# The first RMSNorm of a hybrid decoder layer: its factor leaves the matmul operands and is applied to the products

## The chip, the core and the metric

The kernel runs on one core of a Trainium2 chip. The core has a matrix engine (TensorE, PE in the profile, with PEld for its weight loads), three engines for elementwise work (VectorE or DVE, ScalarE or ACT, GpSimd or POOL) and SyncE (SP), which here issues every DMA. The engines run their own instruction streams and wait for each other by semaphores. The metric is the device time of one execution in microseconds, lower is better. The kernel's matmuls are in fp32r; for accuracy each fp32 product is made from three of them, with each operand split into a high part (rounded to fp32r) and a low part (the rest): high x high, high x low, low x high.

## What is computed

One layer of a decoder for 1088 tokens (1024 of a prompt, 64 of samples), model width 1024. Cut to the part that the change touches:

```python
h = rmsnorm(x, norm1_g)                  # x * rsqrt(mean(x*x) + EPS) * g, per token
z = h @ w_in                             # columns: c_q 384 | c_kv 256 | k_rope 32 | u 512 | v 512
c_kv = rmsnorm(z[..., 384:640], kv_norm_g)
k_r = rope(z[..., 640:672], pos)
q = rmsnorm(z[..., :384], q_norm_g) @ w_q_up
zg = gelu(z[..., 672:])                  # u and v, exact GELU
u = zg[..., :512]
v = layernorm(zg[..., 512:], v_norm_g, v_norm_b)
g = u * (w_s @ v + b)                    # per chunk of 128 tokens, causal
# attention on q, c_kv, k_r; merge, w_out, residual, second norm, SwiGLU, final norm
```

Everything behind these lines is the same in both kernels. `c_kv`, `k_r` and the samples' `v` are outputs too.

## The kernel before

**Layout.** `x1` holds x with the model width on the partitions: 128 partitions x 8 blocks (`KD`) x 1088 tokens. The tokens come in four column groups, `CH1` = 128, 256, 384 and 320 tokens. `hH`/`hL` are the high and low parts of h in the same layout. They are the stationary operands of the v and u products and the moving ones of the rest. `vwH`/`vwL` and `uwH`/`uwL` are the split weights of v and u.

**Norm 1 in the kernel before.** For each group c: ACT squares the group into `sq0` (line 1557). PE adds the squares over the partitions with a matmul against `ones` (`sum_squares`, line 947), which leaves each token's sum in all partitions of PSUM bank 4+c. DVE picks the diagonal (2068), reduces it (2076) and makes mean plus EPS (2078). POOL raises it to -0.5 (`power`, 739). DVE makes diagonal matrices of the factors (2087), and PE spreads them over the partitions (`spread`, 955). DVE then scales each block of x by gain and factor in place (2058), ACT rounds it into `hH` (1548) and DVE subtracts into `hL` (2116).

**The v stage.** PE makes nine token tiles t = 0 to 8 (128 tokens, the last 64); each is 8 blocks of 3 matmuls (lines 939 to 941, 128x512), 24 in all, into bank t % 4. Tile 0 follows the four weight pieces: `w_v` comes in four loads of 512 KB through `raw`, a ring of two slots; POOL rounds a piece into `vwH` (724), DVE subtracts into `vwL` (2102), and the slot's next load waits for that. Tile t >= 4 waits until the GELU of tile t-4 has left its bank. ACT makes the GELU (1596); DVE the statistics (2139 to 2143); POOL the power (780); DVE the LayerNorm (2149 to 2154); ACT the high part `vH`, POOL the low part `vL` (791). Each engine's program is a loop over t with this order written by hand. Into it are set: the spatial weights on POOL at t = 1 (767 to 727), norm 1 of the fourth group on ACT and DVE at t = 2, and the four pieces of the u weights (`U_SPLITS`: at t = 2, 3, 4, 4, POOL then DVE).

**Behind it.** The u stage has the same nine tiles with `uwH`/`uwL`; its tile 0 waits for the GELU of v tile 5, its tile 1 for that of v tile 6, and so on, and for its weight pieces. The spatial matmuls (`spatial`) stand behind u tile 3. The z stage multiplies six weight pieces (`w_in`: c_q, c_kv, k_rope) with `hH`/`hL`, and normalises c_q and c_kv by the same scheme of sums, `columns`, `power` and `diagonals` as norm 1. Then come attention, the output projection, the gated product in loops (Strassen-like, the bulk of the time), and the final norm.

**SP's queue** is one program as well. It issues loads in a written order and waits in it: whatever stands behind a waiting load waits with it.

## Time and profile before

| | us |
|---|---|
| median of 3 runs | 1373.38 |
| lowest and highest run | 1372.34, 1375.17 |
| span of the profiled execution | 1370.6 |
| PE busy in it | 1319.6 (96%) |
| DVE busy in it | 841.9 (61%) |
| first v product of PE | 15.77 |
| first u product of PE | 84.17 |

The span is the profiler's, from first to last instruction; the device time of a run holds a little more at both ends (here 2.8 us to the median). A row of a timeline gives start, duration, engine, line, operation, output<-input, shape, count and, in brackets, the engine's idle time before it and what ended it. Durations of matmuls overlap: the distance of two starts is what one costs in a row of them.

### The profile page before, as it was taken

What the parts mean: (1) busy time and instruction counts of PE and PEld (TensorE: products, weight loads), DVE (VectorE), ACT (ScalarE), POOL (GpSimd) and SP (SyncE); (2) the same over time, 40 slices, a digit from 0 to 9 for tenths busy, and PEclk for the clock granted to TensorE, in tenths of its full rate; (3) what the DMA queues carried; (4) which work ended last, traced back from release to release, by engine and by line L of the source; (5) the groups of instructions that cost most, each with busy time, mean ns of one, the idle gap of its engine ahead of it and who ended that gap; (6) DMA issues with size and microseconds to landing.
All of it is one profiled execution on the core that took longest, in us unless ns stands there. A gap on an engine that the chain in (4) does not pass through costs nothing.

```text
span 1370.6 us, 24016 instructions
## 1 busy us (share of the span) xinstructions
PE 1319.6 (96%) x9436; PEld 1234.7 (90%) x9436; DVE 841.9 (61%) x1284; ACT 508.4 (37%) x886; POOL 432.3 (32%) x279
## 2 busy tenths in 40 slices
PE   6999999999999999899999999999999999999997
PEld 4778998788888667899899999999999999999987
DVE  5896136666666336447965534455445568998976
ACT  3413223665665414112522222222222234544461
POOL 1362333633423204654044444444443410000000
PEclk9999999999999899999999999999999999999998
DMA  7001001100005643642122222222221279757503
GB/s 250 16 31 66 32 31 41 39 1 21 0 19 181 213 173 112 209 149 86 39 80 79 86 72 72 69 77 86 78 86 64 78 276 352 261 190 239 183 1 131
DMA packets 67771, 146.34 MB, mean 107 GB/s; under 512 B 7810, under 2 KB 15362, under 8 KB 67234
## 3 DMA queue, kind: packets, MB, share of 16 engines
q1 hardware_dynamic: 67682, 145.12, 31.2%
q8 instruction: 59, 0.97, 0.3%
q14 instruction: 30, 0.25, 0.1%
HBM read 122.54 MB, written 22.55 MB: 106 GB/s over the span
## 4 chain that ended last, share of the span: by engine, by line
PE 81%; DVE 9%; issue 4%; DMA 2%; ACT 2%; POOL 2%; SPq 0%; POOLq 0%; DVEq 0%; ACTq 0%
PE ps L939 24%; PE ps L940 24%; PE ps L941 24%; PE ps L1179 2%; DMA araw<-in_w_dn 1%; PE ps L947 1%; DVE x L2058 1%; PE ps L1245 1%; POOL rt L739 1%; PE ps L1290 1%; DVE diag L2087 1%; DVE mL L2409 1%; PE ps L955 1%; PE ps L1255 1%; DVE aHL L2720 0%
## 5 line engine op out<-in xcount | busy, mean ns | idle before, releaser
L908 POOL TENSOR_TENSOR ws<-wraw,ws 128x1024 fp32r<-128x1024 f32 x50 | 125.3, 2506 | 214.9 <-ACT ws L1548 214.9
L939 PE MATMUL ps<-bHL,aHL 128*128 128x272 f32 x616 | 178.4, 290 | 4.3 <-DVE bHL L2723 4.1
L941 PE MATMUL ps<-bHL,aHL 128*128 128x272 f32 x616 | 177.3, 288 | 0.0
L940 PE MATMUL ps<-bHL,aHL 128*128 128x272 f32 x616 | 177.1, 288 | 0.0
L2566 DVE TENSOR_TENSOR bufP<-bufP,ps 128x544 f32<-128x544 f32 x66 | 47.4, 720 | 131.9 <-PE ps L941 129.6
L1548 ACT ACTIVATE ws<-wraw 128x1024 fp32r<-128x1024 f32 x55 | 58.4, 1062 | 173.1 <-PE ps L941 169.0
L939 PEld LDWEIGHTS ps<-bHL,aHL 128*128 128x128 f32 x616 | 116.0, 188 | 5.6 <-DVE bHL L2723 5.5
L940 PEld LDWEIGHTS ps<-bHL,aHL 128*128 128x128 f32 x616 | 116.0, 188 | 0.0
L941 PEld LDWEIGHTS ps<-bHL,aHL 128*128 128x128 f32 x616 | 115.9, 188 | 0.0
L931 POOL TENSOR_TENSOR rt<-ms,mhalf 128x3 f32<-128x3 f32 (+1 forms) x3 | 3.0, 997 | 252.7 <-DVE ms L2753 252.7
L2299 DVE TENSOR_TENSOR pTL<-ps,pTH 128x512 fp32r<-128x512 f32 (+1 forms) x96 | 53.2, 555 | 43.3 <-ACT pTH L1548 42.3
L908 POOL TENSOR_TENSOR ws<-wsum,ws 128x1024 fp32r<-128x1024 f32 x20 | 57.3, 2865 | 60.5 <-ACT ws L1548 60.5
L1548 ACT ACTIVATE aHL<-araw 128x512 fp32r<-128x512 f32 x66 | 41.7, 632 | 91.9 <-DVE araw L2695 47.3
L848 POOL TENSOR_TENSOR prob<-prob,rsm 128x128 f32<-128x128 f32 (+5 forms) x48 | 49.6, 1042 | 77.7 <-DVE rsm L2274 77.7
L2566 DVE TENSOR_TENSOR bufC<-bufP,ps 128x544 f32<-128x544 f32 x42 | 30.2, 719 | 69.1 <-PE ps L941 69.1
L1548 ACT ACTIVATE pTH<-ps 128x512 fp32r<-128x512 f32 (+1 forms) x96 | 46.9, 489 | 49.0 <-PE ps L1179 48.0
L1712 ACT ACTIVATE prob<-ps,nmx 128x128 f32<-128x128 f32 (+3 forms) x64 | 47.4, 740 | 24.1 <-DVE nmx L2285 23.9
L2285 DVE TENSOR_REDUCE nmx<-ps 128x1 f32<-128x128 f32 (+3 forms) x64 | 47.7, 751 | 12.6 <-PE ps L1160 12.2
L939 PE MATMUL ps<-x5H,ws 128*128 128x272 f32 x176 | 50.8, 289 | 2.0 <-DVE x5L L2481 1.6
L1179 PE MATMUL ps<-ident,prob 128*128 128x128 f32 x288 | 50.2, 285 | 2.5 <-DVE pTL L2299 1.0
L939 PE MATMUL ps<-x3H,ws 128*128 128x272 f32 x176 | 50.8, 289 | 0.9 <-DVE x3L L2476 0.9
L939 PE MATMUL ps<-x1H,ws 128*128 128x272 f32 x176 | 50.8, 288 | 1.0 <-POOL ws L908 1.0
(365 smaller groups left out, 4561.8 us busy)
## 6 DMA issues: line engine op xcount, KB each, us to landing
araw<-in_w_dn SPq DMA_DIRECT2D x121, 256.0 KB, 3.4
wraw<-in_w_gu SPq DMA_DIRECT2D x44, 512.0 KB, 3.6
cp<-in_cache SPq DMA_DIRECT2D x64, 272.0 KB, 4.8
ab<-acts SPq DMA_DIRECT2D x34, 272.0 KB, 4.9
raw<-in_w_out SPq DMA_DIRECT2D x16, 512.0 KB, 4.2
acts<-bufC SPq DMA_DIRECT2D x22, 272.0 KB, 2.1
x<-x2s SPq DMA_DIRECT2D x8, 544.0 KB, 6.5
x2s<-x SPq DMA_DIRECT2D x14, 272.0 KB, 4.7
```

Source lines behind the costliest of these rows:

```text
L739: pool.tensor_tensor(rt[:, j % 4, :], ms[:, j % 4, :], mhalf[:, :].broadcast_to((P, 3)), ALU.pow).then_inc(nm_pow, 1)
L848: pool.tensor_tensor(row, row, rsm[:, r % 4:r % 4 + 1].broadcast_to((P, n)), ALU.mult).then_inc(s_pn, 1)
L908: pool.tensor_tensor(w[:, 1, :], w_source(j), w[:, 0, :], ALU.subtract).then_inc(cw_lo, 1)
L939: nc.tensor.matmul(out, wh, xh, start=start, stop=False)
L940: nc.tensor.matmul(out, wh, xl, start=False, stop=False)
L941: return nc.tensor.matmul(out, wl, xh, start=False, stop=stop)
L1179: last = nc.tensor.transpose(ps[:, 4 + x % 2, P * qi:P * qi + P], prob[:, at:at + P], ident[:, :])
L1548: return nc.scalar.activation(out, x, ACT.Copy, scale=scale)
L1712: nc.scalar.activation(prob[:, prob_at(qt):prob_at(qt) + n], psf[:, 1024 * (r % 2):1024 * (r % 2) + n], ACT.Exp, bias=nmx[:, s:s + 1], sca ...
L2285: nc.vector.tensor_reduce(nmx[:, s], psf[:, at:at + P * (qt + 1)], AX.X, ALU.max, negate=True).then_inc(s_nm, 1)
L2299: nc.vector.tensor_tensor(pTL[:, x % 4, c0:512], ps[:, 4 + x % 2, c0:512], pTH[:, x % 4, c0:512], ALU.subtract).then_inc(t_free, 1)
L2566: nc.vector.tensor_tensor(halves(out[:, g, :]), halves(x[:, g, :]), pair(b + 2 * g), ALU.add).then_inc(added, 1)
```

## The change

1. **Operands.** `hH` and `hL` are now the two parts of x * g without the token's factor r = rsqrt(mean + EPS). ACT rounds x * g with the gain as its scale (`hi1`); DVE makes the low part with one `scalar_tensor_tensor`, x * g - hH (`low1`). Squares, sums, picks, diagonals and spreads of norm 1 are gone from ACT, PE, DVE and POOL, and so is the scaling pass.
2. **Factor.** A second copy of x in DRAM, `x_tok` (1088 x 1024, tokens on the partitions), is loaded in ten pieces of 512 KB (the ninth overlaps the eighth, the tenth holds the 64 samples, 256 KB) through `xt`, a ring of three slots. ACT squares a piece and adds it up by row (`square_rows`, with `accum_out`) into `ssq1`; DVE makes mean plus EPS in four batches (`mean1`: pieces 0, 1-2, 3-5, 6-9); POOL makes the power (`power1`) into `rv1`, tokens on the partitions.
3. **Where it is applied.** The GELUs of v and u take `rv1` as their per-partition scale. The norms of c_q and c_kv cancel the factor, if EPS is divided by r squared: `columns` adds `eq1` = EPS * q1 instead of EPS. For the key, `rv1` is stored to DRAM (`r_row`, 1088 elements of 4 bytes) and loaded back over 64 partitions (`csr`), where DVE multiplies it by the rotary table `cs`; the key uses `csr`.
4. **Order.** SP's loads stand in another order, ACT's loop has the squares in it, the gelu table is loaded earlier in ACT's program. PE has no norm-1 work in the v stage.
5. Small things: `ident` is loaded with the constants; some semaphores are merged; `dynamic_dma_scratch_size=1024` is given to the builder.

```diff
+XT = 10
+XT_AT = [*range(0, SEQ, P), T - P, SEQ]
+XT_BATCH = (0, 1, 3, 6, XT)
...
+def xt_rows(b):
+    return min(P, T - XT_AT[b])
+def xt_of(t):
+    return t if t < NT - 1 else XT - 1
...
+            def load_xt(b):
+                if b >= 3:
+                    sp_.wait_ge(n1_sq, b - 2)
+                m = xt_rows(b)
+                sp_.dma_start(xt[0:m, b % 3, :], d["x_tok"][XT_AT[b]:XT_AT[b] + m, :]).then_inc(ld_xt[b % 3], 16)
...
+            sp_.wait_ge(n1_pow, len(XT_BATCH) - 1)
+                sp_.dma_start(r_row[0:SEQ].rearrange("(j p) -> p j", p=P), rv1[:, 0:SEQ // P]).then_inc(ld_cs, 16)
+                sp_.dma_start(r_row[SEQ:T].rearrange("(j p) -> p j", p=NS), rv1[0:NS, XT - 1:XT]).then_inc(ld_cs, 16)
             sp_.wait_ge(v_fin, NT)
             sp_.dma_start(d["v_out"], vs[0:NS, :]).then_inc(out_v, 16)
+            sp_.wait_ge(ld_cs, 32)
             sp_.dma_start(cs[:, :], d["cs"]).then_inc(ld_cs, 16)
+            sp_.dma_start(csr[NOPE:P, :], r_row[:].unsqueeze(0).broadcast_to((P - NOPE, T))).then_inc(ld_cs, 16)
...
+            def power1(b):
+                cols = slice(XT_BATCH[b], XT_BATCH[b + 1])
+                pool.wait_ge(n1_mean, b + 1)
+                pool.tensor_tensor(rv1[:, cols], q1[:, cols],
+                                   mhalf[:, :].broadcast_to((P, cols.stop - cols.start)), ALU.pow).then_inc(n1_pow, 1)
...
                 split(N_V + j, gw(vwH, j), None)
-                if j == 0:
-                    power(J_N1)
-            power(J_N1 + 1)
-            power(J_N1 + 2)
-            fold(J_N1 + 3, sq0, KD // 2, CH1[3][1], 0)
-            power(J_N1 + 3)
+            power1(0)
+            power1(1)
...
+                if t == 2:
+                    power1(2)
+                elif t == 4:
+                    power1(3)
...
-            sum1(0)
-            spread1(0)
             for t in range(NT):
                 m, b = rows(t), t % 4
-                if t == 2:
-                    sum1(3)
-                elif t == 4:
-                    spread1(3)
...
-                    if t == 0 and k == KD // 2:
-                        sum1(1)
-                    elif t == 1 and k == KD - 2:
-                        spread1(2)
...
-                if t == 0:
-                    spread1(1)
-                    sum1(2)
...
+            def square_rows(b):
+                m = xt_rows(b)
+                act.wait_ge(ld_xt[b % 3], 16 * (b // 3 + 1))
+                nc.scalar.activation(xt[0:m, b % 3, :], xt[0:m, b % 3, :], ACT.Square,
+                                     accum_out=ssq1[0:m, b:b + 1]).then_inc(n1_sq, 1)
...
+                    act.wait_ge(n1_pow, sum(at <= xt_of(t) for at in XT_BATCH))
+                    nc.scalar.activation(v_tile(t), ps[0:m, t % 4, :], ACT.Gelu,
+                                         scale=rv1[0:m, xt_of(t):xt_of(t) + 1]).then_inc(v_gelu, 1)
...
+            low1(0, range(2))
             weights_lo(N_V, gw(vwL, 0), gw(vwH, 0))
-            factors1(0)
-            norm1(0)
-            for j in range(2, 4):
+            low1(0, range(2, KD))
+            for j in range(1, 4):
                 weights_lo(N_V + j, gw(vwL, j), gw(vwH, j))
-            for c in range(1, 3):
-                factors1(c)
-                norm1(c)
-            factors1(3)
+                if j == 1:
+                    low1(1, range(4))
+                elif j == 2:
+                    low1(1, range(4, KD))
+            low1(2)
+            mean1(0)
+            mean1(1)
...
+            dve.wait_ge(ld_cs, 64)
+            nc.vector.tensor_tensor(csr[NOPE:P, :], csr[NOPE:P, :], cs[NOPE:P, :], ALU.mult).then_inc(kr_a, 1)
```

How the written order moves, at three places. **DVE, the start of the program, before** (`vwL` is a weight piece's low part, `x_102` is `x1`, `g_52` the gain):

```order
L2102 TENSOR_TENSOR vwL<-raw,vwH 128x1024
L2068 TENSOR_TENSOR diag<-ps,ident 128x128
L2076 TENSOR_REDUCE sums<-diag 128x1
L2078 TENSOR_SCALAR ms<-sums 128x1
L2087 TENSOR_TENSOR diag<-ident,rt 128x128
L2058 SCALAR_TENSOR_TENSOR x_102<-x_102,g_52,ps 128x128 x2
L2116 TENSOR_TENSOR hL<-x_102,hH 128x128
```

The same place in the changed kernel (`x_107` is `x1`):

```order
L2136 SCALAR_TENSOR_TENSOR hL<-x_107,g_52,hH 128x128 x2
L2130 TENSOR_TENSOR vwL<-raw,vwH 128x1024
L2136 SCALAR_TENSOR_TENSOR hL<-x_107,g_52,hH 128x128 x6
L2130 TENSOR_TENSOR vwL<-raw,vwH 128x1024
L2136 SCALAR_TENSOR_TENSOR hL<-x_107,g_52,hH 128x256 x4
L2130 TENSOR_TENSOR vwL<-raw,vwH 128x1024
L2136 SCALAR_TENSOR_TENSOR hL<-x_107,g_52,hH 128x256 x4
```

The first two low parts of h stand ahead of the first weight piece now, the factor's steps are gone, and the second group's low parts stand between the weight pieces.

**SP, the start of its program, before:**

```order
L506 DMA x_102<-in_x 128x8x128
L510 DMA ident<-in_ident 128x128
L510 DMA g_52<-in_g 128x8
L502 DMA raw<-in_w_v 128x1024 x2
L506 DMA x_102<-in_x 128x8x256
L506 DMA x_102<-in_x 128x8x384
L502 DMA raw<-in_w_v 128x1024 x2
L519 DMA vgb<-in_vgb 128x1024
```

The same place in the changed kernel:

```order
L524 DMA x_107<-in_x 128x8x128
L534 DMA g_52<-in_g 128x8
L520 DMA raw<-in_w_v 128x1024 x2
L524 DMA x_107<-in_x 128x8x256
L520 DMA raw<-in_w_v 128x1024 x2
L524 DMA x_107<-in_x 128x8x384
L531 DMA xt<-in_x_tok 128x1024 x3
L524 DMA x_107<-in_x 128x8x320
```

The third and fourth weight pieces moved ahead of the third group of x, and three pieces of the token-major copy stand ahead of the fourth group and of all constants.

**ACT, the loop of the v stage, before** (`vf` is a GELU's output):

```order
L1596 ACTIVATE vf<-ps 128x512 x2
L1548 ACTIVATE hH<-x_102 128x320 x8
L1548 ACTIVATE cmaskR<-cmask 128x128
L1548 ACTIVATE identR<-ident 128x128
L1596 ACTIVATE vf<-ps 128x512
L1548 ACTIVATE vH<-vf 128x512
```

The same place in the changed kernel (`rv_77` is `rv1`, `ssq_75` is `ssq1`):

```order
L1584 ACTIVATE xt,ssq_75<-xt 128x1024 x3
L1618 ACTIVATE vf<-ps,rv_77 128x512 x2
L1568 ACTIVATE hH<-x_107,g_52 128x320 x8
L1618 ACTIVATE vf<-ps,rv_77 128x512
L1568 ACTIVATE vH<-vf 128x512
L1584 ACTIVATE xt,ssq_75<-xt 128x1024 x3
L1618 ACTIVATE vf<-ps,rv_77 128x512
```

Three row squares stand ahead of the first GELU, three ahead of the fourth, and four (not shown) ahead of the sixth.

## Rows read from the trace of the kernel before

**Rows 1.** The page's first part: busy time, share of the span, instructions.

```profile
PE 1319.6 (96%) x9436; PEld 1234.7 (90%) x9436; DVE 841.9 (61%) x1284; ACT 508.4 (37%) x886; POOL 432.3 (32%) x279
```

**Rows 2.** The chain that ended last, its first 16 us: start, us, what.

```profile
2.71 5.62 DMA raw<-in_w_v
8.50 1.06 POOL vwH L724
9.69 1.23 DVE vwL L2102
...
15.34 0.29 DVE hL L2116
```

**Rows 3.** The timeline of PE, 0 to 85 us: start, us, engine, line, operation.

```profile
6.72 3.75 PE L947 MATMUL ps<-sq,ones 128*128 128x128 f32 x16 [6.72 <-ACT sq L1557]
...
15.77 0.77 PE L939 MATMUL ps<-vwH,hH 128*128 128x512 f32 x1 [1.20 <-DVE hL L2116]
...
16.34 0.63 PE L940 MATMUL ps<-vwL,hH 128*128 128x512 f32 x1
...
20.60 0.63 PE L941 MATMUL ps<-vwH,hL 128*128 128x512 f32 x1
...
21.80 3.78 PE L947 MATMUL ps<-sq,ones 128*128 128x256 f32 x16 [0.57 <-DVE vwL L2102]
...
40.76 0.94 PE L955 MATMUL ps<-diag,ones 128*128 128x128 f32 x6 [2.60 <-DVE diag L2087]
...
56.59 0.48 PE L939 MATMUL ps<-vwH,hH 128*128 128x512 f32 x1
...
84.17 0.39 PE L939 MATMUL ps<-uwH,hH 128*128 128x512 f32 x1
```

**Rows 4.** Busy time of lines 947 and 955, 0 to 60 us, summed.

```profile
sum 60.00, PE 15.18 PEld 10.98; mean PE 3.04 PEld 2.20
...
sum 60.00, PE 3.27 PEld 2.59; mean PE 0.65 PEld 0.52
```

**Rows 5.** Groups by form, 0 to 84 us, and timeline rows of POOL, ACT, DVE.

```profile
L2154 DVE TENSOR_TENSOR vf<-vf,vgb 128x512 f32<-128x512 f32 x4 | 5.7, 1430 | 0.1
L2102 DVE TENSOR_TENSOR uwL<-raw,uwH 128x1024 fp32r<-128x1024 f32 x3 | 5.8, 1943 | 0.0
L1548 ACT ACTIVATE hH<-x 128x384 fp32r<-128x384 f32 x8 | 4.2, 526 | 6.8 <-DVE x L2058 6.8
L2058 DVE SCALAR_TENSOR_TENSOR x<-x,g,ps 128x320 f32<-128x320 f32 x8 | 4.2, 534 | 0.0
...
59.43 2.51 POOL L727 TENSOR_TENSOR spL<-raw,spH 128x1024 fp32r<-128x1024 f32 x1
...
77.79 0.58 ACT L1596 ACTIVATE vf<-ps 128x512 f32<-128x512 f32 x1
...
83.67 0.58 ACT L1596 ACTIVATE vf<-ps 128x512 f32<-128x512 f32 x1
...
104.73 1.66 DVE L2154 TENSOR_TENSOR vs<-vs,vgb 64x512 f32<-64x512 f32 x1
```

**Rows 6.** DMA: one stretch of 3 us (last two columns share, GB/s); a wait; a landing.

```profile
12.00:15.00 3.00, 0.79 (x2) 0.50 (x2) 1.51 (x3) 0.01 (x1) 1.59 (x2) 1.00 1.07 377
...
18.04 1.05 POOL L724 TENSOR_SCALAR vwH<-raw 128x1024 fp32r<-128x1024 f32 x1 [4.45 <-DMA raw<-in_w_v]
...
raw<-in_w_u SPq DMA_DIRECT2D x4, 512.0 KB, 3.6
```

**Rows 7.** The timeline of ACT: its first square, 1024 columns, behind the load of x.

```profile
5.52 1.06 ACT L1557 ACTIVATE sq<-x 128x1024 f32<-128x1024 f32 x1 [3.44 <-DMA x<-in_x]
```

**Rows 8.** A DMA issue with its landing, POOL's timeline, and DVE in a stretch (0.00).

```profile
x<-in_x SPq DMA_DIRECT2D x1, 512.0 KB, 4.7
...
119.32 1.04 POOL L724 TENSOR_SCALAR w0H<-raw 128x1024 fp32r<-128x1024 f32 x1
...
160.00:180.00 20.00, 20.00 (x124) 20.00 (x123) 0.00 (x0) 4.75 (x7) 3.84 (x3) 1.00 0.15 53
```

220 lines of the change are left out of this document (114 added, 106 removed).

## The prediction, made before the changed kernel was run

> **What bounds the kernel now.** I read the busy shares first: PE is busy for 96% of the span, DVE for 61% [rows 1]. So a change pays if it takes work or waiting from PE's own stream, and what happens on the other engines counts only where PE waits for them. Then I read the chain that ended last and PE's timeline in the part that the change touches. In the chain [rows 2] the first weight piece lands, is rounded and has its low part at 9.69 + 1.23 = 10.9 us, but PE's first product starts only at 15.77 [rows 3]: between lie diagonal, power, spread and scaling, the norm's factor. In PE's timeline the sums (line 947) and spreads (955) of norm 1 stand between the products, 15.18 and 3.27 us of busy time [rows 4], with one more wait of 2.60 us for a diagonal [rows 3]. From 56.59 to the first u product at 84.17 there is nothing but products: 5 tiles of 24 in 27.58 us, 5.52 us a tile, 0.230 us a product. From there into the z stage PE hardly waits in its timeline, and what follows in the u and z stages is timed by what PE has done. So I need one number: when the first u product starts. The rest of the kernel moves by the same amount.
>
> **Start of PE.** The two parts of x * g need only the first group of x and g. The load of x lands at 5.5 [rows 7]; two high and two low parts, each under the 0.53 us of the wider ones [rows 5], are ready by 7.6, before the weights. So the first product starts when the first weight piece is ready: 10.9, say 11.0, which is 4.8 us earlier.
>
> **Tile 0** takes its products in four portions of 6, one per weight piece. The early products before cost (20.60 - 16.34) / 10 = 0.426 us each [rows 3], against 0.230 later: the first at TensorE's lower clock level (1.2 GHz), the later ones at the upper (2.4), though the granted clock is given as 1.00 for an early stretch too [rows 6]. Portion 1: 11.0 to 13.6. The second piece landed with the first; DVE makes six low parts (an estimate of 0.34 each for 128 columns, from 0.534 for 320 [rows 5]; 2.0 us), then the piece (1.23 [rows 2]): ready at 14.2 at the latest. Portion 2: 14.2 to 16.8. The third piece is issued when its slot is free (10.9). Before, it landed only at 18.0 [rows 6], behind 2.5 MB of x at up to 377 GB/s; now the third group of x stands behind it, and I take the 3.6 us of a piece that has the queue to itself [rows 6]: 14.5. POOL 1.05 to 15.6; DVE, behind four low parts of 256 columns (an estimate of 0.47 by the same row), ready at 17.3. The fourth piece, issued at 14.2, lands at 17.8, POOL to 18.9, DVE behind four more low parts to 20.4. Portion 4 then ends at 21.8 at the upper level, 23.0 at the lower. With the low parts overlapping a little (0.1 us each) it would be 21.1. I take 21.7.
>
> The row shows that 3.75 us of work at the lower level, from 6.72, did not raise the clock, and that it stood at the upper level from about 22, after products from 15.77 on. The Trainium skill ("TensorE: Matmul & The Clock Gate", Part 1) says that a throttled clock is the default and that sustained matmul activity releases it; by that the small gaps between my four portions could hold it down longer. The sum would be 1.2 us worse for portion 4, and up to 2.5 more if the next tile's first dozen are slow too.
>
> **Tiles 1 to 8.** Tile 1 needs the second group (low parts done at 19.2), tile 3 the third, tile 6 the fourth. No norm work stands between them: 8 x 5.52 = 44.2 us if nothing is late. First u product: 21.7 + 44.2 = **65.9**, against 84.17: 18.3 us earlier. Cross-check by what leaves PE: behind 15.77 stood 15.18 - 3.75 of sums and 3.27 - 0.79 of spreads, 13.9 us, and 2.6 us of waiting; tile 0 costs about 10.7 now where its products alone cost 12 x 0.426 + 12 x 0.230 = 7.9. 13.9 + 2.6 - 2.8 = 13.7, with 4.8 of the start 18.5. The two agree.
>
> **Is something late?** Loads: the third group of x is issued behind the fourth weight piece at 14.2 and lands at about 21.5 at 370 GB/s; ACT's 8 high parts (0.53 each [rows 5]) are done at 25.5, DVE's low parts at 26, tile 3 needs them at 32.7. Three pieces of the token-major copy land by 25.7, the fourth group by 29.5, the constants by 32. ACT squares a piece in 1.06 us [rows 7]: three until 28.5. Batch means and powers (0.9 us each) are done by 29.5; the GELU of tile 0 is at 28, of tile 1 at 30. PE needs them at 38.3 and 43.8. The fourth group (ACT from 29.5) is ready on DVE by 40.5; it was 7.0 us of scaling and subtracting, now 8 instructions that lie near the 0.534 of the 320-wide one [rows 5]; tile 6 needs it at 49.3.
>
> The tightest chain is the one through all engines. Pieces 3 to 5 of the copy are issued from 26, behind them the spatial weights, which land at about 37.5. POOL works on these until 43.5, 2.51 us of it in one instruction [rows 5]; DVE's instructions with two SBUF inputs stretch beside such work (a weight piece at line 2102 takes 1943 ns on average [rows 5] and 1.23 us with POOL idle [rows 2]; line 2154 takes 1430 [rows 5]), which I count. DVE ends tile 1's norm at 44.8 and the first u piece at 46.5, then comes the third mean (46.7), POOL's power (47.6) and the GELU of tile 3 at 48.3: PE needs it at 54.8, 6 us of room. DVE then needs what it needed before, 5.88 us for a tile and a u piece by the distance of two GELUs that waited for it (77.79 and 83.67 [rows 5]). ACT reaches the last four squares at about 52.6; the tenth piece is issued behind the seventh square, lands at 56.5, and the GELU of tile 5 ends at 58.6. The first u product waits for it at 65.9: 7 us. The fourth u piece is ready at 61.6, needed at 70.0. The GELU of tile 6 waits for the last power (62.6), needed at 71.4. So the program has 6 to 8 us of room at each meeting, and PE should wait nowhere. DVE ends the LayerNorms at about 79.5 where it was 104.73 + 1.66 = 106.4 [rows 5]; the spatial products need them at 87.7.
>
> **What is added later.** The row squares, ten of 1.06 us plus an accumulator read, are on ACT, which has the room. The store of `r_row` waits for the last power (62.6) behind all u loads; `csr` and `cs` come behind v's last norm (79.5) and ahead of the six w_in pieces. POOL takes the first w_in piece at 119.32 before [rows 8], so at 101 now: nothing there unless the store takes over 30 us. The product for `csr` (1088 columns, under the 1430 ns x 2 of two stretched instructions of 512 [rows 5]) lies in DVE's idle time; DVE was wholly idle from 160 to 180 [rows 8]. The norms of c_q and c_kv change one short instruction of 3 columns into another: between -0.1 and +0.1 us on each of six links, taken as zero. The GELU's scale from a column instead of a constant: its 0.58 us [rows 5] could become 0.5 to 0.7, beside PE's work, so zero.
>
> The Trainium skill ("DMA: Bandwidth & Descriptors", Specifications) asks for transfers of at least 512 B for line rate and has shorter ones do a read-modify-write. No row here has a four-byte run; the rule gives no price, and by the sum above it moves nothing while the store is within its room.
>
> **Sum.** 1373.38 - 18.4 (between the two countings, 18.3 and 18.5) = **1355.0 us**. Against the profiled execution: 1370.6 - 18.4 = 1352.2 of span, plus the 2.8 us that lie around it.
>
> **Rivals.**
> - *The factor comes late.* The chain of tile 3's or tile 5's GELU through loads, squares, mean and power is later than its room of 6 to 8 us. For: it crosses five engines and a ring of three slots, each of my times is a sum of some ten terms, and DVE was behind PE in this stage before: the GELU of tile 5 started at 77.79 [rows 5], 6.4 us ahead of its need at 84.17. Against: DVE loses its scaling pass. Being 9 to 12 us late gives the first u product at 68 to 71: 1357 to 1361.
> - *A better start.* The clock rises early and the pieces come quickly: tile 0 ends at 20.5, 1353.8; if in addition waits in the z stage happen to close, 1352.5.
> - *The gain is given back.* The u or z stage is bound by an engine that kept its own time. For: DVE ended the v stage only at 106.4, 22 us behind the first u product. Against: that end moves by 27 us, more than PE. It would give 1360 to 1370; at its end the change doesn't do what it says, and the factor's work only sits elsewhere.
> - *Slower, by the store of `r_row`.* 1088 runs of four bytes, and SP waits for them with the w_in pieces behind. The nearest row is the first load of x, 1024 runs of 512 B in 4.7 us [rows 8]. If the store took over 42 us, POOL would hold the powers of the u stage behind a missing w_in piece, and PE would lose one for one; from 63 us on the kernel is slower. At 70 ns a run, 76 us, it would be 1355 + 34 = 1389. That is sixteen times the row's price.
>
> **Chances.** Forecast (1353.5 to 1357) 0.70; late factor 0.14; better start 0.06; given back 0.07; slower 0.03. A difference of 0.2%, 2.7 us, is about what a measurement of this kernel tells from none: faster 0.95, same 0.02, slower 0.03. The range takes in the better start and the late factor, and leaves out about 0.12: 1352.5 to 1361.
>
> **What would show it.** Right: first product at 11, tile 0 done by 22, first u product near 66, no wait of PE over 1 us between, DVE's last LayerNorm near 80, and PE's busy time 18 us less. Wrong: PE waiting for an ACT GELU at 49 to 72 us (the late factor), products at 0.43 us behind 24 us (the clock), a wait for `w0H` at 124 (the store), or an unchanged start of attention.

## The result, and the profile after

The changed kernel takes 1363.45 us in the median of 4 runs (1359.54 to 1364.8), the kernel before 1373.36 beside it; the ratio is 0.9931, 95% interval 0.9917 to 0.9944. So it is faster, by 9.9 us where 18.4 were forecast, and 2.5 us outside the range. The profiled execution has a span of 1360.7 us (1362.44 with what lies around it). In both kernels 1.7 us lie around the span of a run; the 2.8 us of the table before set the profiled run's span against the time of another run.

PE's busy time, the row that answers to [rows 1], fell from 1319.6 to 1308.5, by 11.1 and not by 18. Second row: the granted clock in 40 slices, in tenths.

```profile
PE 1308.5 (96%) x9362; PEld 1226.2 (90%) x9362; DVE 821.2 (60%) x1241; ACT 513.0 (38%) x902; POOL 429.2 (32%) x279
...
PEclk9999999999999899899999999999999999999998
```

PE's timeline, against [rows 3]. The four rows with an idle time are the starts of tile 0's four portions.

```profile
10.45 0.77 PE L983 MATMUL ps<-vwH,hH 128*128 128x512 f32 x1 [10.45 <-DVE vwL L2130]
...
13.89 0.80 PE L983 MATMUL ps<-vwH,hH 128*128 128x512 f32 x1 [0.55 <-DVE vwL L2130]
...
17.39 0.80 PE L983 MATMUL ps<-vwH,hH 128*128 128x512 f32 x1 [0.57 <-DVE vwL L2130]
...
20.89 0.80 PE L983 MATMUL ps<-vwH,hH 128*128 128x512 f32 x1 [0.57 <-DVE vwL L2130]
...
25.75 0.63 PE L985 MATMUL ps<-vwH,hL 128*128 128x512 f32 x1
26.18 0.45 PE L983 MATMUL ps<-vwH,hH 128*128 128x512 f32 x1
...
68.50 0.39 PE L983 MATMUL ps<-uwH,hH 128*128 128x512 f32 x1
```

The starts are those of the forecast: 11.0, 14.2, 17.3, 20.4 were expected. But twelve products from 20.89 to 26.18 cost 0.44 us each, and only from 26.18 on do they cost 0.227. The first u product stands at 68.50, 15.7 us earlier than before; 65.9 was forecast. PE's waits from 0 to 110 us (in total, times, the longest):

```profile
PE ps L983 <- DVE vwL L2130: 12.1, 4, 10.4
```

So PE waits for nothing but the four weight pieces. The engines behind it (ACT's square and accumulator read, the GELUs of tiles 3 and 5, the last LayerNorm, the first w_in piece, the key's table), in ACT's, DVE's and POOL's timelines:

```profile
28.30 0.18 ACT L1584 ACTIVATION_READ_ACCUMULATOR xt<-xt 128x1 f32 x1
28.39 1.04 ACT L1584 ACTIVATE xt<-xt 128x1024 f32<-128x1024 f32 x1
...
51.61 0.69 ACT L1618 ACTIVATE vf<-ps,rv 128x512 f32<-128x512 f32 x1 [8.90 <-POOL rv L776]
...
62.65 0.67 ACT L1618 ACTIVATE vf<-ps,rv 128x512 f32<-128x512 f32 x1
...
83.75 1.66 DVE L2187 TENSOR_TENSOR vs<-vs,vgb 64x512 f32<-64x512 f32 x1
...
131.03 3.34 DVE L2243 TENSOR_TENSOR csr<-csr,cs 64x1088 f32<-64x1088 f32 x1
...
103.57 1.06 POOL L760 TENSOR_SCALAR w0H<-raw 128x1024 fp32r<-128x1024 f32 x1
```

And the small transfers of the factor, 60 to 100 us (KB each, median us to landing):

```profile
csr<-r_row SPq DMA_DIRECT2D x1, 272.0 KB, 5.5
...
r_row<-rv SPq DMA_DIRECT2D x1, 4.0 KB, 9.5
r_row<-rv SPq DMA_DIRECT2D x1, 0.2 KB, 10.5
```

Where the rest went is read from the starts of the first product of each stage. Stretches in us, first execution of each kernel; "n160" is a kernel of the experiments (`n_fetch160`) that does the work of the changed one:

```
stretch                                          before    after     n160
start to first u product                          84.17    68.50    68.13
u stage and z stage                              146.93   146.87   146.90
to the attention's first probabilities            23.73    24.46    24.48
attention                                        196.71   196.49   196.53
samples, to their first product with the cache    19.62    20.37    18.60
to the output projection                          57.78    57.78    57.79
output projection, to the second norm's sums      60.65    61.65    60.66
second norm, to x0 of the gated product           52.96    52.92    51.36
gated product, x0 to x6                           43.01    43.02    43.02
gated loop, from x6 on                           428.61   429.73   428.63
down projection                                  214.89   217.47   215.22
final norm                                        41.54    41.44    41.39
first u product to the end                      1286.43  1292.20  1284.57
```

The u and z stages took what they took. The changed kernel loses 0.7 at the start of attention, 0.8 in the samples' part, 1.0 in the output projection, 1.1 in the gated loop and 2.6 in the down projection, and gains 0.4 in the others: 5.8 us in all are given back, in stages whose instructions are the same.

### The profile page after: what moved, and what is told of

Same layout as the page of the kernel before. It is cut to its first block, busy times and chain, and to the rows that moved or that the text cites. A ratio compares the mean times of both kernels' runs of the same rounds, so it can differ in the third digit from the quotient of the medians.

```text
span 1360.7 us, 23850 instructions
## 1 busy us (share of the span) xinstructions
PE 1308.5 (96%) x9362; PEld 1226.2 (90%) x9362; DVE 821.2 (60%) x1241; ACT 513.0 (38%) x902; POOL 429.2 (32%) x279
## 4 chain that ended last, share of the span: by engine, by line
PE 80%; DVE 8%; issue 5%; DMA 3%; ACT 2%; POOL 2%; SPq 0%; POOLq 0%; DVEq 0%; ACTq 0%
PE ps L983 24%; PE ps L984 24%; PE ps L985 24%; PE ps L1199 2%; DMA araw<-in_w_dn 2%; PE ps L1265 1%; DVE x L2082 1%; PE ps L991 1%; DMA ab<-acts 1%; PE ps L1310 1%; POOL rt L782 1%; DVE mL L2446 1%; DVE hL L2136 1%; PE ps L1275 1%; DVE aHL L2757 0%
```

## The experiments

All were timed in five rounds, beside runs of the kernel before (medians 1372.3 to 1373.4). "Rest" is the median less the 1.7 us around the span and less the first u product of the kernel's profile. As that product comes from one execution (67.57 to 68.50 in three of the changed kernel), a rest is good to about 1 us.

### The two kernels again, and a frame without the change

**The changed kernel a second and a third time.** (`a_after`, `p_after`)

> The changed kernel again. In its first trace the first u product starts at 68.50 us, 15.7 us earlier than before, but the end comes only 9.9 us earlier: 5.8 us are given back, about 0.7 at the start of attention, 0.6 in the samples' part, 1.1 in the output projection, 1.1 at the start of the gated loop, 2.6 in the down projection. Theory 1 (chance of that one execution: the spells of low clock and DMA landings differ from one execution to the next): the median of more runs is near 1373.4 - 15.7 = 1358 us, between 1357 and 1360, and the shifts of the parts differ in the new trace. Theory 2 (lasting: something of the change costs time late in the program): again 1362 to 1364, and the same parts give the same amounts back.

1363.88 us (6 runs), ratio 0.9934 (0.9914 to 0.9954); first u product 67.57, the stretch behind it 1295.0. The same parts give time back, three of them in other amounts: 0.7 us at the start of attention, 1.1 in the samples' part, 0.7 in the output projection, 2.6 in the gated loop, 3.8 in the down projection.

> The changed kernel unchanged, beside the three others on one chip. Median 1362 to 1365, first u product 67.5 to 68.5, loop entry 429.7 (x6 to the down projection), down projection 217.5 to 218.7, a fetch 1.5 to 1.75 us behind the issue of the load at the loop's entry, which lands after 5.1 to 5.4 us. If it comes out at 1357 here, the differences to the kernels with waits were between chips and not between kernels.

1362.04 us (6 runs), ratio 0.9915 (0.9897 to 0.9933). In three sets, 16 executions in all, the changed kernel's rest is 1292.4 to 1294.6: the loss is lasting. Not all its parts are: the down projection takes 217.5 and 218.7 us in the first two profiles but 216.0 in this one, under what was expected. And single executions last from 1357.16 to 1366.17 us. Their mean granted clock goes with that: it is 0.984 in the seven of 1363.4 to 1366.2 us, 0.985 or 0.986 in the eight of 1359.5 to 1363.4, and 0.989 in the one of 1357.16.

**The kernel before again.** (`a_before`)

> The kernel before again, for a second trace of it: how much the stretches between the same two matmuls differ between two executions of one kernel. Theory 1: single stretches (start of attention, samples' part, output projection, down projection) differ by 0.5 to 2.5 us from the first trace, the time stays at 1373 to 1375 by the median. Theory 2: the stretches repeat within 0.3 us.

1372.92 us (12 runs), ratio 1.0004 (0.9994 to 1.0014), rest 1287.5. Nine of the eleven stretches behind the first u product repeat within 0.3 us; the samples' part is 0.4 us shorter and the output projection 0.7 longer.

**The kernel before with the change's DRAM tensors and scratch size, unused.** (`c_frame`)

```
+        r_row = nc.dram_tensor("r_row", (T,), F32).ap()
-    arr = {"x": ...}
+    arr = {"x": ..., "x_tok": x}
-    nc = bacc.Bacc(...)
+    nc = bacc.Bacc(..., dynamic_dma_scratch_size=1024)
```

> The kernel before with the changed kernel's surroundings alone: the second copy of x and the row of factors exist in DRAM, but nothing loads or stores them, and the builder has the smaller scratch for dynamic DMA. Every engine's instructions are those of before. If the place of the tensors in DRAM or the scratch costs what was given back late, this runs 3 to 6 us slower than before (1376 to 1379). If neither matters: 1373 to 1374.

1372.73 us (12 runs), ratio 0.9998 (0.9987 to 1.0009). Placement in DRAM and scratch size cost nothing. In its profile the first u product stands at 85.33, 1.2 us later than in the kernel before with the same instructions; the clock was low from 13.3 to 20.1 and from 40.6 to 44.0 us.

### The early clock

**Filler products** (`b_warm`; 128x128 of ones into a free bank), 24 before tile 0 and 6 in each weight wait:

```
+            fill(24, 4)
             for t in range(NT):
...
+                        if k:
+                            fill(6, 5)
                         pe.wait_ge(split_lo, N_V + k // 2 + 1)
```

> The changed kernel with matmuls that serve nothing on PE, ones by ones into free banks: 24 ahead of the first v product and 6 in each of the three waits for a weight piece. Clock theory: PE's products in tiles 0 and 1 cost 0.43 us until 26 us because PE had done too little before; kept busy from 1 us on, they cost 0.23 from about 11 us, tile 0 ends near 22.3, and the first u product starts at 66 to 66.5 where it was 68.5; the time falls by 2 to 2.5 us. Rival (the clock follows the time since the start, not the work): products stay at 0.43 until 26, the filling costs 3 x 1 us or more, the first u product is at 70 to 73 and the kernel 2 to 5 us slower than the changed one.

1351.58 us (5 runs), ratio 0.9851 (0.9832 to 0.987). The first u product came at 66.23, as expected. But the total fell by 12.3 us and not by 2.3; its rest is 1283.7. (The profile has two records for each filler.)

**Only the 24 ahead of tile 0:** (`f_head`)

> The changed kernel with only the 24 filler products before tile 0, none in the three weight waits. Those waits (0.55 to 0.57 us each in the changed kernel) come back. If short waits with a quarter of tile 0 between them keep the granted clock at its lower level, the products of tile 0 stay at 0.43 us until about 26 us and the first u product stands at 68 to 68.5; if the early work alone raises it, it stands at 66.5 to 67. Behind it: theory A (shift alone) gives 1292 to 1295 at 68.5 and an open number at 66.5; theory B (early work) gives 1286 in either case. Totals: 1353 for B, 1361 to 1364 for A at 68.5.

1354.02 us (4 runs), ratio 0.9859 (0.9839 to 0.988). PE's timeline of this kernel:

```profile
1.05 8.43 PE L1008 MATMUL ps<-ones 128*128 128x128 f32 x48 [1.05 <-POOL ms L794]
10.17 0.50 PE L983 MATMUL ps<-vwH,hH 128*128 128x512 f32 x1 [0.69 <-DVE vwL L2136]
...
13.67 0.71 PE L983 MATMUL ps<-vwH,hH 128*128 128x512 f32 x1 [1.84 <-DVE vwL L2136]
14.18 0.63 PE L984 MATMUL ps<-vwL,hH 128*128 128x512 f32 x1
...
20.72 0.50 PE L983 MATMUL ps<-vwH,hH 128*128 128x512 f32 x1 [1.88 <-DVE vwL L2136]
21.06 0.40 PE L984 MATMUL ps<-vwL,hH 128*128 128x512 f32 x1
```

Portions 1, 3 and 4 have their products at 0.23 us; portion 4 starts within 0.2 us of the changed kernel's. Portion 2, behind a wait of 1.84 us, is slow again, at 0.43 (granted clock 0.50 from 13.8 to 17.2 us); in `b_warm`, with fillers in the waits, it is not. The first u product stands at 66.20.

**All weight waits ahead of the first product:** (`e_late`)

```
-                    if t == 0 and k % 2 == 0:
-                        pe.wait_ge(split_lo, N_V + k // 2 + 1)
+                    if t == 0 and k == 0:
+                        pe.wait_ge(split_lo, N_V + 4)
```

> The changed kernel with one change: the first product of tile 0 waits for all four pieces of w_v_in, not for the first alone, so TensorE starts at 20.9 and then works without a wait. If the lower clock level then lasts the same time from there (until about 26), the first u product stands at 72 to 73 (18 products of 0.227 more behind 68.5). If the three waits had held the level low until 26, it rises earlier here, and the product stands at 71 to 72. Behind it: theory A (shift) gives a number of its own, between 1285 and 1296, not bound to 1292; theory B (no early work) gives 1292 or more. Totals: 1358 to 1368.

1361.85 us (6 runs), ratio 0.9914 (0.9898 to 0.9931). Its timeline:

```profile
20.06 0.77 PE L983 MATMUL ps<-vwH,hH 128*128 128x512 f32 x1 [20.06 <-DVE vwL L2130]
...
22.33 0.63 PE L985 MATMUL ps<-vwH,hL 128*128 128x512 f32 x1
22.76 0.47 PE L983 MATMUL ps<-vwH,hH 128*128 128x512 f32 x1
```

PE starts 9.6 us later than in the changed kernel and has its products at full pace 3.4 us earlier, after six products without a wait. The first u product is at 70.55, even ahead of the expected 71 to 73. So in the changed kernel portions of 2.6 to 2.9 us with idle 0.55 to 0.57 us between them went with the lower level (1.2 GHz) until 26 us; working early or without a pause ended it sooner. Eight of the profiles have this tile 0 unchanged: in seven the level rises at 24.9 to 26.3 us, in the eighth (`h_fetch96`, below) at 13.2. That is where the 2.6 us ahead of the u stage went; it is what mostly happens, not what must.

### What is given back behind the first u product

**The fillers and 13 more behind tile 0** (`g_shift`), meant to put the first u product back to where the changed kernel has it:

```
                 last.then_inc(v_ready, 1)
+                if t == 0:
+                    fill(13, 5)
```

> The kernel with filler products (24 small ones before tile 0, 6 in each of its three weight waits; the first u product at 66.2, from there to the end 1285.8) with 13 more of the same 128x128 products of ones behind tile 0. At 0.17 to 0.18 us each they should move the first u product by 2.3 us to about 68.5, where the changed kernel has it, while TensorE still never stands still from 1 us on. Theory A (what the changed kernel loses behind the first u product depends on where its later idle spells fall in time, so on the shift alone): the stretch from the first u product to the end comes out near the changed kernel's 1292 to 1295 us, the total near 1361 to 1364. Theory B (it depends on whether TensorE ran early and was not left standing in tile 0): the stretch stays at 1286, the total is 1354. Theory C, an early feeding of something else that the fillers did by chance: neither number is bound.

1358.06 us (6 runs), ratio 0.9892 (0.9871 to 0.9913); first u product 69.46, the stretch behind it 1285.7, rest 1286.9. It overshot by 1 us, so it isn't the changed kernel's very moment, and the total lies between those of theories B and A; but the stretch is that of theory B: a later first u product doesn't by itself bring the loss back.

**No work for the factor.** (`d_nofactor`) No token-major copy is loaded and no row squared; a constant stands for the mean squares.

```
-                sp_.dma_start(xt[0:m, b % 3, :], d["x_tok"][...]).then_inc(ld_xt[b % 3], 16)
-                nc.scalar.activation(xt[0:m, b % 3, :], xt[0:m, b % 3, :], ACT.Square,
-                                     accum_out=ssq1[0:m, b:b + 1]).then_inc(n1_sq, 1)
```

> The changed kernel without the nine loads of the token-major x and without ScalarE's nine row squares; the mean square of every token is a constant instead, and everything behind it (factor columns, GELUs with them, the row stored and read back, the rotary table) stays. So the output is not the reference's. The first u product should stay at 68 to 68.5, since TensorE has no wait between 20.9 and there. Theory D (the work for the factor costs time behind, by its transfers or ScalarE's time): the stretch to the end falls from 1292 to 1286, the total to 1354 to 1356. Theories A and B: it stays within 1 us of the changed kernel, 1361 to 1364, unless the first u product moves too.

1359.18 us (6 runs), ratio 0.99 (0.988 to 0.9919), first u product 68.24, rest 1289.3. It fell between the two expectations. The gated loop and the down projection of its profile take 429.7 and 218.1 us, as slow as the changed kernel's; so the factor's work doesn't make these slow.

**Waits that wait for nothing.** The fillers did one thing more: they added instructions to PE's program. The four next kernels add nothing else but such instructions, waits on a semaphore that has long been up:

```
                 for k in range(KD):
+                    for _ in range((0, 3, 3, 3, 3, 2, 2, 2, 2)[t]):
+                        pe.wait_ge(made, 1)
                     last = mm3(...)
```

This one adds 160; with 1, 2 or 4 per block it is 32, 96 or 256.

> The changed kernel with 96 more waits in TensorE's program, each on a semaphore that has long been up, spread over tiles 1 to 8 of the v stage (two ahead of each three products in tiles 1 to 4, one in tiles 5 to 8). They take no work and no transfer. The trace shows TensorE's instructions fetched in blocks of 16 KB, one each 15 to 16 us of the gated loop, and each fetch is a transfer: in the four profiles that lose 2.22 us at the gated loop's entry (the changed kernel twice, the one with all weight waits ahead, the one without factor work) one falls 1.5 to 3.75 us behind the issue of the 512 KB weight load there, within its flight, in the five others outside. Theory E (where the fetches fall among the large loads decides, and the change moved it by taking 148 instructions out of TensorE's program): 96 more put the fetches where the kernel with the early fillers has them, so the loop's entry costs nothing (x0 to first product of the down projection 427.5 to 428 behind x6, not 429.7), the down projection takes 215.3 to 216, not 217.5, and the median falls from 1363.7 to 1358 to 1360, while the first u product stays at 67.5 to 68.5. Theory B (what counts is whether TensorE worked early): nothing moves, 1362 to 1365.

1357.39 us (5 runs), ratio 0.9897 (0.988 to 0.9914). Its profile is an odd one: the clock rose in the second portion.

```profile
13.11 0.54 PE L983 MATMUL ps<-vwH,hH 128*128 128x512 f32 x1 [0.54 <-DVE vwL L2132]
13.49 0.40 PE L984 MATMUL ps<-vwL,hH 128*128 128x512 f32 x1
```

So the first u product stands at 65.44, and the profiled execution, 1352.01 us, is 5.4 us under the median. Up to there TensorE's program is that of the changed kernel, portions and pauses too, so these alone don't settle when the level rises. The fetch fell 0.7 us ahead of the load's issue, and the load still landed after 4.8 us; the loop takes 428.6 us.

> The changed kernel with 256 such waits, four ahead of each three products in tiles 1 to 8. 256 is about the number of instructions in one block of 16 KB, so the fetches behind the v stage fall where the changed kernel has them. It is the control for the waits themselves. Theory E: nothing is gained, loop entry 429.7, down projection 217.5, median 1362 to 1366 (up to 2 us more if four waits and six instructions do not fit into the 0.68 us of three products). If the waits as such speed something up, it falls like the one with 96.

1356.76 us (4 runs), ratio 0.9881 (0.9863 to 0.9898), first u product 68.55, rest 1286.5. As a control it failed: the fetch came 4.0 us ahead of the load and not 1.5 behind it, and 5 to 7 us were gained where none was expected (the changed kernel has 1362.04 to 1363.88).

> The changed kernel with 160 idle waits (three and two ahead of each three products in tiles 1 to 4 and 5 to 8). The fetch should fall 2 to 4 us ahead of the load's issue, and the next 10 us behind it, so outside its flight. Theory E: loop entry 427.5, down projection 215 to 217, median 1355 to 1359.

1354.71 us (4 runs), ratio 0.9866 (0.9851 to 0.9881), first u product 68.13, rest 1284.9. This is the changed kernel with idle waits alone, 7.3 us faster than the changed kernel on the same chip, and the intervals don't meet. The fetch fell 2.7 us ahead of the load's issue, and the load landed after 3.8 us; the loop takes 428.6 us, not 427.5.

> The changed kernel with 32 idle waits (one ahead of each three products in tiles 1 to 4). With 96 the fetch came 2.25 us earlier against the load, with 256 it came 5.75 us earlier. 32 should bring it 0.7 to 2 us earlier than 1.5 us, so to the load's first microsecond or just ahead of it. Theory E (fetches among the loads): between the changed kernel and the one with 96, loop entry 428.6 to 429.7, median 1358 to 1363. A theory by which any idle wait helps by itself gives 1357 as with 96 and 256.

1361.7 us (5 runs), ratio 0.9913 (0.99 to 0.9925), rest 1292.3: no gain. The fetch fell 0.6 us behind the issue, and the load landed after 4.7 us. So it isn't any wait that helps. Theory B (working early) falls too: `k_fetch256` and `n_fetch160` have no early work, and their rest is that of the kernel before or less.

**The fetch aimed at the load's flight**, in three ways:

> The kernel with 24 filler products ahead of tile 0 (median 1354.0, fetches outside the load at the gated loop's entry) with 136 more such waits in tiles 1 to 8. At about 16 instructions per us of the gated loop the fetch that fell 10.5 us behind the load's issue should fall about 2.5 us behind it, within its flight, as in the changed kernel. Theory E: the first u product stays at 66.2, the loop's entry loses 2.2 us (429.7), the down projection 2 to 3 (217.5 to 218), the median rises to 1357 to 1359. Theory B: TensorE works early all the same, so 1353 to 1355.

1354.93 us (4 runs), ratio 0.9878 (0.9862 to 0.9893): not slower. The fetch fell 8.7 us behind the load's issue, not 2.5, and the load landed in time (3.6).

> The kernel before with 112 such waits in tiles 1 to 8 of its v stage. Its fetch at 9.5 us behind the issue of that load should come 7 us earlier, so about 2.5 us behind it, within its flight. Theory E: the stretch from x6 to the down projection rises from 428.6 to 429.7 or more, the down projection from 214.7 to 217 or more, the median from 1373.0 to 1375 to 1377: the kernel before would show what the changed one shows. Theory B: no change, 1372 to 1374.

1372.7 us (11 runs), ratio 1.0004 (0.9995 to 1.0013): not slower. The fetch fell 3.7 us behind the issue, just as the load had landed (3.7). In its profile the first u product stands at 86.82, 2.7 us later than in the kernel before, with the granted clock low from 40.1 to 46.9 us, and the stretch behind it takes 1283.8.

```
-                    nc.tensor.matmul(ps[:, bank, 0:P], ones[:, :], ones[:, :], start=True, stop=True)
+                    nc.tensor.matmul(ps[:, bank, 0:32], ones[:, :], ones[:, 0:32], start=True, stop=True)
...
-            fill(24, 4)
+            fill(58, 4)
```

> Ahead of tile 0 58 filler products of 32 columns stand in place of 24 of 128 columns (median 1354.0), 34 products and so 136 instructions more in TensorE's program, over by about 10 us as well. At 16 instructions per us of the gated loop the fetch 10.5 us behind the issue of the load at the loop's entry comes 8.5 us earlier, to about 2 us behind it, within its flight. Theory E: that load lands after 5 us and not 3.7, the loop's entry costs 429.7 and not 427.5, the down projection 217 or more, and the median is 1357 to 1359, with the first u product at 66.2. If the fetches do not matter: 1353 to 1355.

1363.85 us (6 runs), ratio 0.9935 (0.9917 to 0.9953). The first u product stands at 76.34 and the rest is 1285.8. The fetch fell 3.0 us behind the issue, and the load landed after 3.8 us: the expected loss is missing. The fillers took far longer than estimated:

```profile
1.05 24.96 PE L1008 MATMUL ps<-ones 128*128 128x32 f32 x116 [1.05 <-POOL ms L794]
25.82 0.77 PE L983 MATMUL ps<-vwH,hH 128*128 128x512 f32 x1
...
28.86 0.39 PE L984 MATMUL ps<-vwL,hH 128*128 128x512 f32 x1
```

A record of 32 columns costs 0.215 us here, one of 128 columns in `f_head` 0.176. And TensorE counts as busy for 25 us without a pause, yet the first six products behind it cost 0.43 us each, the lower level; in `f_head` those at 10.2 us were at the upper one.

### What the traces show at the places of the loss

**The load at the gated loop's entry.** The changed kernel: SP's queue, ACT, PE, and the transfers from 677.1 to 682.2 us.

```profile
677.12 0.43 SPq L639 DMA_DIRECT2D wraw<-in_w_gu  x1
...
682.21 1.06 ACT L1568 ACTIVATE ws<-wraw 128x1024 fp32r<-128x1024 f32 x1 [2.09 <-DMA wraw<-in_w_gu]
...
686.75 0.39 PE L983 MATMUL ps<-x1H,ws 128*128 128x272 f32 x1 [2.06 <-POOL ws L952]
...
GB/s 0 0 0 119 324 427 375 410 393 394 161 161 193 289 225 225 386 482 386 321 418 308 248 406 354 376 324 324 152 66 68 32 32 32 32 32 137 444 358 461
...
q8 instruction: 1, 0.02, 1.2%
...
wraw<-in_w_gu SPq DMA_DIRECT2D x1, 512.0 KB, 5.1
```

The same load in `f_head`, where these 4 us have no row of an instruction queue:

```profile
675.09 0.43 SPq L639 DMA_DIRECT2D wraw<-in_w_gu  x1
...
678.80 1.06 ACT L1574 ACTIVATE ws<-wraw 128x1024 fp32r<-128x1024 f32 x1 [0.72 <-DMA wraw<-in_w_gu]
...
wraw<-in_w_gu SPq DMA_DIRECT2D x1, 512.0 KB, 3.7
```

In the first, a fetch of one block of instructions (16 KB) 1.7 us behind the issue, and at the end five steps of 32 GB/s: nearly everything has landed, a small rest hasn't. ACT gets the load 1.4 us later, POOL makes the low part later, and PE waits 2.06 us where it waits nothing in the other. In 18 profiles the fetch fell between 0.75 us ahead of this load's issue and 3.75 us behind it in nine; in seven of these the load landed after 4.7 to 5.8 us (the changed kernel three times, `d_nofactor`, `e_late`, `m_fetch32`, `h_fetch96`), in two after 3.7 and 3.8 (`j_before112`, `l_head58`). In the nine others it landed after 3.6 to 3.9.

All 720 such loads from x0 on (40 in each of the 18 profiles) say where in the flight a fetch counts:

```
fetch against the load's issue        loads   landed after 4.6 us or more
0.8 us ahead to 1.5 us behind            39    9
1.5 to 2.7 us behind                      8    8
2.7 to 3.9 us behind                     40    1 (`e_late`, 3.85 behind)
none of these                           633    0 (median 3.5)
```

So late landings come with a fetch in the flight's first 2.7 us, and the two placements aimed at the flight, at 3.0 and 3.7 us behind the issue, missed that part. No run brought a late landing on purpose. But idle waits took one away: the fetch is 1.7 to 1.8 us behind the issue in the changed kernel (landed after 5.0 to 5.4), 0.6 behind with 32 waits (4.7), 0.7 ahead with 96 (4.8), 2.7 ahead with 160 (3.8) and 4.0 ahead with 256 (3.6).

What the landing costs is PE's wait at the loop's entry: nothing where the load landed after 3.6 to 3.7 us (seven profiles), 0.97 us after 3.8 to 4.8 (six, among them the kernel before twice, `h_fetch96` and `m_fetch32`), and 2.06 us after 5.0 to 5.9 (the changed kernel three times, `d_nofactor`, `e_late`). The stretch from x6 on takes 427.5, 428.6 and 429.7 us with them, and 431.2 in two of the changed kernel, where the clock fell once more behind the wait.

**The lower clock level behind the same pause.** In the output projection PE waits 4.46 us for DVE in every kernel. Changed kernel, then n160:

```profile
546.26 0.57 PE L983 MATMUL ps<-mH,w0H 128*128 128x272 f32 x1 [4.46 <-DVE x L2458]
...
551.61 0.43 PE L985 MATMUL ps<-mH,w0L 128*128 128x272 f32 x1
551.84 0.34 PE L983 MATMUL ps<-mH,w0H 128*128 128x272 f32 x1
552.02 0.29 PE L984 MATMUL ps<-mL,w0H 128*128 128x272 f32 x1
```

```profile
544.21 0.56 PE L983 MATMUL ps<-mH,w0H 128*128 128x272 f32 x1 [4.46 <-DVE x L2460]
...
547.52 0.32 PE L985 MATMUL ps<-mH,w0L 128*128 128x272 f32 x1
547.67 0.29 PE L983 MATMUL ps<-mH,w0H 128*128 128x272 f32 x1
```

The products behind it are at 0.225 us for 5.6 us in the one and for 3.3 us in the other, then at 0.125: half of the 2.3 us' difference, about 1 us, is lost (61.65 against 60.66 above). Over 18 profiles the lower level ends 3.3 to 6.0 us behind the pause; 4.9 to 5.7 in the three of the changed kernel. It lasts 3.4 us in eight profiles, and the stretch then takes 60.6 to 60.7 us, or 6.8 us in ten, and it takes 61.2 to 61.8. The kernel before has one profile of either kind, so this differs between executions of one kernel too.

In the samples' part it is the same. The first product of that part to the first with the cache, changed kernel and n160:

```profile
436.33:456.70 20.37, 18.52 (x103) 13.15 (x102) 6.15 (x11) 9.52 (x18) 0.73 (x1) 0.75 0.60 218
436.03:454.63 18.60, 15.67 (x101) 12.14 (x100) 6.06 (x11) 9.42 (x18) 0.73 (x1) 0.91 0.66 239
```

The granted clock (last but two) is 0.75 in the one and 0.91 in the other: at the lower level for 10.2 and 3.4 us. The kernel before has 10.2 us too and takes 0.8 us less than the changed one, so that part of the loss isn't a longer spell. The start of attention takes 23.7 us in the six profiles with 3.4 us of it (the kernel before twice) and 24.0 to 24.5 in the twelve with 6.8 (the changed kernel three times). From the first u product to the final norm the lower level takes 20.5 us in the first profile of the kernel before, 27.3 in that of the changed one and 13.7 in that of n160.

The second place has no pause at all. Here the squares are summed by products of one column. The changed kernel's stretches of 4 us (second number: PE busy; last but two: granted clock), then those of n160:

```profile
574.00:578.00 4.00, 4.00 (x37) 4.00 (x35) 0.44 (x1) 0.55 (x1) 2.76 (x2) 1.00 0.57 209
578.00:582.00 4.00, 4.00 (x24) 4.00 (x24) 0.17 (x1) 0.00 (x0) 1.34 (x1) 0.66 0.85 315
```

```profile
572.00:576.00 4.00, 4.00 (x36) 4.00 (x35) 0.59 (x2) 0.00 (x0) 1.80 (x1) 1.00 0.58 180
576.00:580.00 4.00, 4.00 (x35) 4.00 (x34) 1.02 (x3) 0.48 (x1) 2.36 (x2) 1.00 0.73 265
```

PE counts as busy throughout; in the one its clock is granted at 0.66 behind the sums, and some 15 products take twice their time (52.92 against 51.36 us for this stretch), in the other not. Either the one or the other happens: the stretch is 51.36 to 51.39 in six profiles and 52.92 to 52.98 in twelve, and nothing between.

## Why the prediction was right and wrong

**Start of PE, right.** 10.45 us for 11.0. The portions' starts, the path of the weight pieces through POOL and DVE and the landing behind the third group of x came within 0.6 us.

**Tile 0 and 1, mis-sized.** The step was "21.7" for the end of tile 0, with the later portions "at the upper level". The clock remark beside it (1.2 us for portion 4 and up to 2.5 with the next tile's first dozen) named the mechanism and left it out of the sum. Measured: 12 products at 0.44 from 20.89, 5.29 us instead of 2.76, and the first u product 2.6 us later than the sum. In the kernel before the level rose at 22 us behind twelve products without a pause ([rows 3], 15.77 to 21); the change cut that run of twelve into portions of six with pauses between them. The Trainium skill ("TensorE: Matmul & The Clock Gate", Part 1) has a throttled clock released by sustained matmul activity; `e_late` and `f_head` agree with it. The longer low spell should have been in the sum with its price, though `h_fetch96` shows that it doesn't come in every execution.

**Nothing is late, right, with worse numbers.** GELU of tile 3 at 51.61 (48.3 forecast), of tile 5 at 62.65 (ended by 58.6 forecast), last LayerNorm ended at 85.4 (79.5). The spatial weights reach POOL at 40.8 (37.5 forecast) and are done at 46.9 (43.5); the chain behind them runs 3 to 6 us later than summed; the room of 6 to 8 us took it. The first u product had 5 us left, not 7. The rival of the late factor didn't come.

**Added later, right.** The store landed within 10.5 us, far from the 42 at which it would decide. The first w_in piece is taken by POOL at 103.57 (101 forecast). The square is 1.04 us and 0.18 for the accumulator read; the GELU with a column for its scale is 0.67 to 0.69 us against 0.58, the upper end of what was given; the key's product is 3.34 us where "under" 2.9 was said. None is on PE's path.

**"The rest of the kernel moves by the same amount", wrong.** This is the step that failed. 5.8 us are lost behind the first u product, and the time came to where the rival "the gain is given back" had it (1360 to 1370), but not by its mechanism: the u and z stages kept their length to 0.1 us. What the runs show in its place: the part behind the first u product isn't one number. It is 1284 to 1295 us, kernel by kernel and in part execution by execution, with the same work, by how long PE's lower clock spells last and by when large loads land. Adding idle waits to PE's program moves it by up to 7.4 us (`m_fetch32` to `n_fetch160`). The kernel before sits at 1287, the changed one, by its placement, near the top at 1292 to 1295. Of the 5.8 us the longer clock spells at the start of attention and in the output projection are 1.7 and the wait at the loop's entry 1.1; the 2.6 of the down projection are PE's waits in part (6.3 us against 4.2) and vary (1.1 in the third profile). That last placement is not owed to the change's design: with 160 or 256 idle waits the changed kernel takes 1354.7 and 1356.8 us. That 1354.7 is near the forecast 1355.0 is luck: its first u product is 2.2 us later than forecast, and its rest lies 2.6 us under that of the kernel before.

**What stays open.** Of the 7.6 us between the changed kernel's profile and that of n160, 2.6 are in the two spells of the output projection, 1.1 in the gated loop's entry, 2.3 in the down projection and 1.8, of clock again, in the samples' part. So 4.3 us go with the clock's spells and 3.4 are elsewhere, 1.1 of them the late load's. That PE's program is the handle is shown. That instruction fetches are the way by which it acts on the loads is argued from the 720 loads and from the idle waits that took a late landing away; of the placements aimed at a late one none hit the part of the flight where they occur. What delays the down projection isn't settled. How the lengths of the clock spells come about isn't either; they follow neither a later start alone (`g_shift`) nor early work alone (`k_fetch256` and `n_fetch160` have none and lose nothing).

**A better version.** The changed kernel with the fillers ahead of and within tile 0 takes 1351.58 us, 1.5% less than the kernel before and 0.9% less than the changed one; some 2 us of it are the earlier full clock, the rest goes with its placement, which no run tells apart from the fillers' own work. Its interval meets that of the kernel with 160 idle waits (0.9851 to 0.9881), so the two aren't told apart either.

## What to carry to other kernels

A weight-bound start in short portions can cost more than its waits: here the whole of it ran at the lower clock in seven of eight profiles. Give TensorE something to do from the first microsecond (24 products of ones, 128 columns wide, brought the first u product 1.4 to 2.3 us forward; 58 of 32 columns kept it busy to 25.8 us and gained nothing), or start later and without pauses, which here lost only 2 to 3 us for a start 9.6 us later. And when a change of 1% is judged on one program, time it again with some idle instructions in the queue of the engine that bounds it: here that alone moved the time by 0.5%. Read more than one profile, too: one execution of the changed kernel differs from another by up to 9 us.

## What the runs showed of the hardware that was not expected

- TensorE's program is fetched while it runs: 58 blocks of 16 KB over the span on a queue of their own ("q8 instruction"), one each 13 to 30 us, none from 758 to 1026 us, where the gated loop turns. That the queue is TensorE's is read from how idle waits in its program moved the fetches. Of the 720 loads of 512 KB in the gated product of 18 profiles, eighteen landed after 4.6 to 5.9 us (median 3.5), and all eighteen have such a fetch between 0.8 us ahead of their issue and 3.9 us behind it, seventeen within 2.7 us.
- A wait on a semaphore that is already up cost no time that could be seen (first u product 68.13 with 160 of them and 68.55 with 256, 67.6 to 68.5 without), yet it moves what comes 600 us later.
- The granted clock can fall with PE busy all the time: 0.66 over 4 us behind sums by products of one column, in 12 of 18 profiles.
- Behind one and the same pause of 4.46 us the lower level goes on for 3.3 to 6.0 us.
- Products of 32 columns kept PE busy from 1.05 to 25.8 us and the clock stayed at its lower level, to 28.7 us.
- A store of 1024 four-byte runs landed in 9.5 us.
